# Norms of a two-block transformer kernel: the inverse deviations reach the rows by a product with the column repeated as the weight, and a square root stands ahead of the projecting stages

## The reference

```python
def rmsnorm(x, g):
    return x * lax.rsqrt(jnp.mean(x * x, axis=-1, keepdims=True) + RMS_EPS) * g

for i in range(2):                                    # first block
    sh1, sc1, g1, sh2, sc2, g2 = split(silu(c) @ ada_w[i] + ada_b[i], 6)
    h = rmsnorm(x, mix_g[i]) * (1 + sc1) + sh1
    x = x + g1 * (pool_mixer(h) if i == 0 else sgu_mixer(h))
    h = rmsnorm(x, mlp_g[i]) * (1 + sc2) + sh2
    x = x + g2 * (square(relu(h @ w1[i])) @ w2[i])
x = rmsnorm(x, final_g)
h = rmsnorm(x, norm_gain_2)                           # second block
q, k, v, gates = split(h @ w_in_2)                    # 8 heads attend to all, 8 to a neighbourhood
x = rmsnorm(x + (attention(q, k, v) * silu(gates)) @ w_out_2, final_norm_gain_2)
```

## Time and profile before

| what | value |
|---|---|
| median of 3 runs | 2731.51 us (2728.12 to 2732.54) |
| the profiled execution: its time | 2729.32 us |
| its span, first to last instruction | 2727.5 us |
| mean granted TensorE clock | 0.977 |
| PE busy | 2614.6 us (96%) |
| DVE busy | 1379.8 us (51%) |
| ACT busy | 915.1 us (34%) |
| POOL busy | 285.0 us (10%) |
| HBM traffic | 92 GB/s over the span |

### The profile page before, as it was taken

How to read it: one execution, slowest core, us unless ns; L and a number is a source line. 1 busy time by engine, 2 the same in 40 slices (tenths; PEclk the granted TensorE clock), 3 DMA queues, 4 the chain that set the end, 5 groups by cost and what they waited for, 6 DMA issues and landing times.

```text
span 2727.5 us, 34329 instructions
## 1 busy us (share of the span) xinstructions
PE 2614.6 (96%) x12380; PEld 2109.5 (77%) x12380; DVE 1379.8 (51%) x2179; ACT 915.1 (34%) x1437; POOL 285.0 (10%) x278
## 2 busy tenths in 40 slices
PE   7989999999999899899999999999999999998987
PEld 2468888888887898777888888888777897886666
DVE  2765454646445324425343534434651224998963
ACT  2442222222223312224223222222422124887741
POOL 2110000000002000010000000000010002556621
PEclk9999999999999999899999999999999999999998
DMA  8612323232101610312111111110324453346521
GB/s 299 230 62 78 108 77 108 77 108 90 64 31 71 167 53 1 124 54 70 47 46 46 47 45 62 44 49 0 108 77 125 147 144 85 93 104 162 156 78 62
DMA packets 179476, 245.24 MB, mean 90 GB/s; under 512 B 55728, under 2 KB 136752, under 8 KB 179376
## 3 DMA queue, kind: packets, MB, share of 16 engines
q1 hardware_dynamic: 179376, 243.92, 28.8%
HBM read 210.33 MB, written 39.58 MB: 92 GB/s over the span
## 4 chain that ended last, share of the span: by engine, by line
PE 86%; DVE 6%; issue 4%; ACT 2%; POOL 2%; DMA 1%; DVEq 0%; POOLq 0%; SPq 0%; ACTq 0%
PE banks L1666 23%; PE banks L1667 23%; PE banks L1668 23%; PE banks L1746 3%; PE banks L2012 2%; PE banks L2030 2%; DVE Hlo L1338 1%; PE banks L1853 1%; PE banks L1854 1%; PE banks L1855 1%; PE banks L2000 1%; PE banks L1999 1%; PE banks L1696 1%; DMA stage<-ada_w 1%; POOL SUM L773 1%
## 5 line engine op out<-in xcount | busy, mean ns | idle before, releaser
L1666 PE MATMUL banks<-Hhi,Whi 128*128 128x512 f32 x1792 | 715.7, 399 | 17.7 <-ACT TB L1018 6.0
L1667 PE MATMUL banks<-Hlo,Whi 128*128 128x512 f32 x1792 | 704.9, 393 | 0.0
L1668 PE MATMUL banks<-Hhi,Wlo 128*128 128x512 f32 x1792 | 704.7, 393 | 0.0
L1386 DVE SCALAR_TENSOR_TENSOR X<-banks,mod,X 128x512 f32<-128x512 f32 x512 | 381.0, 749 | 206.8 <-PE banks L1668 204.4
L1666 PEld LDWEIGHTS banks<-Hhi,Whi 128*128 128x128 f32 x1792 | 341.7, 191 | 97.7 <-issue 8.7
L1666 PE MATMUL banks<-Mhi,Whi 128*128 128x512 f32 x1024 | 401.5, 392 | 0.0
L1668 PE MATMUL banks<-Mhi,Wlo 128*128 128x512 f32 x1024 | 399.4, 390 | 0.0
L1667 PE MATMUL banks<-Mlo,Whi 128*128 128x512 f32 x1024 | 399.4, 390 | 0.0
L1667 PEld LDWEIGHTS banks<-Hlo,Whi 128*128 128x128 f32 x1792 | 341.9, 191 | 74.2 <-issue 4.2
L1668 PEld LDWEIGHTS banks<-Hhi,Wlo 128*128 128x128 f32 x1792 | 340.9, 190 | 72.7
L896 ACT ACTIVATE Whi<-stage 128x2048 fp32r<-128x2048 f32 x93 | 177.4, 1907 | 553.8 <-PE banks L1668 539.2
(11 more groups left out here) (170 smaller groups left out, 2909.4 us busy)
## 6 DMA issues: line engine op xcount, KB each, us to landing
stage<-w SPq DMA_DIRECT2D x64, 1024.0 KB, 5.5
stage<-ada_w SPq DMA_DIRECT2D x48, 1024.0 KB, 5.3
stage<-w_in SPq DMA_DIRECT2D x13, 1024.0 KB, 6.4
stage<-sgu_in SPq DMA_DIRECT2D x8, 1024.0 KB, 6.3
x_saved<-X SPq DMA_DIRECT2D x16, 512.0 KB, 2.7
X<-x_saved SPq DMA_DIRECT2D x16, 512.0 KB, 7.1
QS<-q_heads SPq DMA_DIRECT2D x32, 256.0 KB, 4.2
KH<-k_heads SPq DMA_DIRECT2D x32, 256.0 KB, 5.3
```

What stands on the lines that cost most here:

```text
L1386: nc.vector.scalar_tensor_tensor(out=X[:, k, half(hf)], in0=Dn[:, i % D_BANKS, :], scalar=gate[:, k:k + 1], in1=X[:, k, half(hf)], op0=ALU ...
L1666: nc.tensor.matmul(out_bank, whi, xhi, start=start, stop=False)
L1667: nc.tensor.matmul(out_bank, whi, xlo, start=False, stop=False)
L1668: return nc.tensor.matmul(out_bank, wlo, xhi, start=False, stop=stop)
```

## The change

The diagonal matrices go away. PE takes each of the four columns of `rstd`, repeated 128 times along the row by a step of zero, as a weight, and streams the identity past it: four products of 128x128 into the four pieces of the bank, in place of one of 128x512. The semaphores `diag_ready` and `r1_diag` go with the diagonals; the reciprocal now waits for the spread before it, and PE waits for the reciprocal itself. A second edit stands in ACT's `project`: at the first of the four stages (j == 0) it takes the root of a constant into a new tile `root`, which nothing reads. The tile `root` takes 32 bytes ahead of `c_act`, and the place of `acc` is fixed where it was relative to `t_at`, so SUM moves down into the bytes of `diag`, and the 2,048 bytes behind it stay unused.

```diff
+    root = sb("root", [P, 1])
     c_act = sb("c_act", [P, KT])
...
-    diag = sb("diag", [P, H])
     SUM = sb("SUM", [P, H])
-    acc_at = top[0]
+    acc_at = top[0] = t_at + 16 * S
...
             def project(T, j, gate, first, then=None):
+                if j == 0 and then is not None:
+                    act.wait_ge(set_ready, 6)
+                    nc.scalar.activation(root[:], epsc[:, 0:1], ACT.Sqrt)
...
                 dve.wait_ge(std_ready, T("n", hf + 1))
-                reach(dve, diag_ready, T("n", hf))
+                reach(dve, rstd_ready, T("n", hf))
                 nc.vector.reciprocal(rstd[:], std[:]).then_inc(rstd_own, 1)
-                dve.wait_ge(rstd_own, T("n", hf + 1))
-                reach(dve, rstd_ready, T("n", hf))
-                if T.n["n"] == 0:
-                    dve.wait_ge(const_loaded, 16)
-                for t in range(4):
-                    ins = nc.vector.tensor_scalar(out=diag[:, t * P:(t + 1) * P], in0=con("ident"),
-                                                  scalar1=rstd[:, t:t + 1], scalar2=None, op0=ALU.mult)
-                ins.then_inc(diag_ready, 1)
...
             def spread(T, hf, bank):
-                pe.wait_ge(diag_ready, T("n", hf + 1))
-                nc.tensor.matmul(bank, ones[:], diag[:], start=True, stop=True).then_inc(rstd_ready, 1)
+                pe.wait_ge(rstd_own, T("n", hf + 1))
+                if T.n["n"] == 0:
+                    pe.wait_ge(const_loaded, 16)
+                along_columns(bank).then_inc(rstd_ready, 1)
+
+            def along_columns(bank):
+
+                for t in range(4):
+                    ins = nc.tensor.matmul(bank[:, t * P:(t + 1) * P], rstd[:, t:t + 1].broadcast_to([P, P]),
+                                           con("ident"), start=True, stop=True)
+                return ins
...
             def first_rstd(hf):
-                pe.wait_ge(r1_diag, hf + 1)
-                nc.tensor.matmul(A[:, hf, :], ones[:], diag[:], start=True, stop=True).then_inc(r1_ready, 1)
+                pe.wait_ge(r1_own, hf + 1)
+                along_columns(A[:, hf, :]).then_inc(r1_ready, 1)
```

More of the change, by code:

```diff
@@ L300, in build @@
     x_rescaled = sem("x_rescaled")
-    r1_own, r1_diag, r1_ready = sem("r1_own"), sem("r1_diag"), sem("r1_ready")
-    rstd_own, diag_ready, rstd_ready = sem("rstd_own"), sem("diag_ready"), sem("rstd_ready")
+    r1_own, r1_ready = sem("r1_own"), sem("r1_ready")
+    rstd_own, rstd_ready = sem("rstd_own"), sem("rstd_ready")
     row_ready, row_copied = sem("row_ready"), sem("row_copied")
@@ L1462, in first_rstd @@
             def first_rstd(T, hf):
-                reach(dve, r1_diag, hf)
+                reach(dve, r1_ready, hf)
                 nc.vector.reciprocal(rstd[:], std1[:, hf, :]).then_inc(r1_own, 1)
[L1466 to L1471, removed]
             def rescale(T, j):
```

## The result

| | before | changed |
|---|---|---|
| median of 5 runs each, side by side | 2732.54 us (2728.12 to 2733.55) | 2715.39 us (2711.38 to 2717.59) |
| ratio, with its 95% interval | | 0.9942 [0.9931, 0.9953] |
| span of the profiled execution | 2727.5 us | 2713.2 us |
| mean granted clock of TensorE | 0.977 | 0.979 |

The medians differ by 17.15 us, the spans by 14.3. The forecast was 17.2 us and 2714.3 us. In two later sets of runs the same kernel took 2715.46 and 2712.90 us, at ratios of 0.9942 [0.9928, 0.9955] and 0.9931 [0.9918, 0.9944].

The account below looks back on a forecast made before the run. The prediction took PE, 86% of the chain, as the bound, with short waits at the norms. Its terms summed to 17.2 us, giving 2712.1 us for the profiled execution and 2714.3 us for the median, range 2708 to 2722.

Parts of the forecast that it names:

- Norm 2, first half: PE's idle time of 1.07 us ahead of the spread goes: 1.1 us gained.
- The clock terms: Behind the removed waits in norm 1, norm 3 and the last norm PE's clock stays up: 1.5, 1.0 and 1.0 us.
- the rival that the clock doesn't stay up: The three gains from a higher PE clock fail, leaving 13.7 us of gain, 2717.8 us; chance 0.22.
- the term "1.5": Norm 1, work behind the first half's spread: no stretch at granted clock 0.50, so 1.5 us gained.
- norm 1's first half: The spread starts at about 143.06 instead of 145.81, 2.75 us gained, and the clock stays up behind it, 1.5 us.
- The new product: Four 128x128 products on PE replace one of 128x512: +0.04 us per spread, 0.4 us over nine on the path.
- The moved tiles: Rival: big tiles shifted by 32 bytes are read or written more slowly everywhere; 1% of PE's time gives 2740 us; chance 0.06.
- Gains given back: Rival: product stages that start earlier find their weights late, so within 5 us of before, 2728 us; chance 0.06.
- The root costs nothing: In ACT's `project`, the new root and its load (1.28 us and some 0.2) fall into ACT's idle time.
- norms 3 and the last: First halves: without table load and diagonals, PE's own sums become the bound; spreads start 2.0 and 1.7 us earlier.
- Second halves: Norms 1 to 4, DVE from reciprocal to next scaled tile: 0.87 us gained each, 3.5 in all.

Follow-up runs that it names:

- kernel 12: The changed kernel run a third time, against the kernel before: 2712.90 us, ratio 0.9931.
- Kernel 7: The changed kernel with each of the four narrow products issued twice: 2723.97 us, 0.9974 of the kernel before.
- Kernel 6: The changed kernel with diagonals and wide product put back for the first half of every norm alone: 2721.60 us, 0.9962 of the kernel before.
- kernel 4: The kernel before with an unused tile of 32 bytes in the place of `root`, so only addresses move: 2731.68 us, ratio 0.9999.
- Kernel 3: The changed kernel with `root` made 64 bytes long: 2711.90 us, 0.9932 of the kernel before.
- kernel 5: The changed kernel with diagonals and wide product put back for the second half of every norm: 2720.50 us, 0.9959 of the kernel before.
- kernel 1: The changed kernel without the early root of a constant, the tile `root` kept: 2717.28 us, 0.9949 of the kernel before.

## Why the prediction was right

**The order of reading.** Idle time (23.6 us) was not taken for gain; each norm's chain was. The local gains are 18.2 us against 17.25, and eleven of the twelve places came within 0.2 us. The medians of the three sets agree with the forecast to 1.1, 1.2 and 1.4 us, which is closer than the sum deserves: 1.6 us or so were given back behind norm 1, the local gains were 0.9 larger than the sum, and medians of one kernel differ by up to 2.6 us between sets.

**Norm 2, first half**: 1.1 forecast, 1.87 measured between the two executions. The wait itself was 1.07 us and is gone, so the step was right. The other 0.8 us is mostly a matter of where a low stretch ends. Before, PE's products between the reciprocal's tile and the spread ran at 0.50 for 1.5 us; in the changed kernel at 0.94. Other profiles of the changed kernel have 1.05 and 0.97 us from reciprocal to spread instead of 0.67. The low stretch is about as long in both and only ends elsewhere, so most of what the one place gains the stretch ahead of it loses.

**The clock terms** were what I was least sure of. In norm 3 and the last norm the changed kernel's spreads take 1.13 to 1.14 us in place of 2.04 to 2.05, but for one of the six in its three profiles: 1.27 us in norm 3 of kernel 12, where the clock fell towards its end. Kernel 7's last norm is the other exception (3.5 us for 2.0). So the rival that the clock doesn't stay up is refuted as the rule, and the term holds in most executions and not in each. In norm 1 the 1.5 us came where they were forecast, and about as much (1.6 to 1.7) was lost again 27 us behind the spread, at a wait that I had not looked at. **This is the step that failed**: the term "1.5" was taken as a gain of the chain to the end, while PE came to the wait for TB earlier and a new drop followed it, in all three profiles of the changed kernel. Net of it, norm 1's first half was worth about 2.5 us (2.66 of wait), not 4.25. Kernel 6 shows besides that the wait ahead of the spread does not always bring the drop.

**The new product** was taken at +0.04 us a spread. In norm 4 it takes 1.00 us where the wide one took 0.96, and in norm 1 1.13 for 1.10. Doubling it added 0.89 us. By the rule of the TensorE page of the Trainium skill (LDWEIGHTS) on columns it would be an estimate of 0.64 us more for each spread, had no load been hidden. The 0.04 us of norm 4 show that nearly all of it is.

**The moved tiles** cost nothing that shows (kernel 4), so the rival on the slower side is refuted. Kernel 3 shows that a third placement has shorter transfers, which no rival had. **Gains given back**: as I put it, by weights that come late, it did not happen; ACT's wait for the weights of `sgu_out` was 14.6 us before and 14.9 in the changed kernel, within the 13.7 to 15.2 of the others. The prediction said that only these weights were waited for; the trace before also has 12.9 us in which PE waits for the modulation's (`ada_w`), all ahead of the opening norm, so nothing in the sum hangs on it. It happened in another way and in a small size, by the clock behind norm 1.

**The root costs nothing** on ACT, as forecast, and the way it works was right: without it the load stands between the square and `std`. Its worth depends on the other edit, 4.2 us alone and 1.9 beside it. The prediction summed both edits together in norms 3 and the last, which was right, but did not say how they share the gain.

**Second halves**: 0.91 us each in place of 0.87, and kernel 5 lost 5.0 us by undoing them, where the local gains are 2.73 + 0.92 + 0.82 = 4.5.

## What to carry to other kernels

For an operation that only prepares an operand of a matmul, ask whether the matmul can read the raw value instead: a column repeated by a zero step was as fast as a dense weight here, and four narrow products for one wide one cost 0.04 us. Read a wait's worth from the releasing instruction to the waiting one, not from the idle time just before it, as the work in between may be running at the low clock; and where a gain makes an engine reach its next wait sooner, look at what follows that wait too. Where two edits shorten the same wait, undo each alone: their gains do not add (4.2 and 1.9 us for the same three lines).

## What was not expected of the hardware

- Behind PE's wait for TB the granted clock fell to 0.50 in all seven profiles in which PE had idled 3.08 to 3.29 us, costing about 1.6 us, and in none of the seven with 1.24 to 2.57 us. At another wait it fell behind 2.11 us in one profile and stayed up behind 2.78 in another.
- The same wait of 3.15 us ahead of a product was followed by a stretch at the 0.50 level in three profiles and by none in a fourth (8.30, 8.30 and 8.36 us of following work, against 6.77). Between executions the heads stage takes 92.8, 94.5 or 96.1 us, as one more stretch at 0.50 or a longer one falls into it.
- Four DVE products of 128x128 took 2.62 us beside POOL's work in norm 1 (kernel 6), 1.88 in the opening norm before, and 0.87 us in norm 1's second half (kernel 5).
- A table load of 1.28 us is followed by its root at once: the load starts at 1210.12 and `std` at 1211.41 in kernel 1.
- `root` at 64 bytes in place of 32 goes with shorter transfers in two profiles (5.3 us for 1 MB of weights where the twelve others have 5.5 or 5.6, 2.0 for the last stores where they have 2.1 to 2.3), with spans 6 us shorter and with a mean 3 us lower. A shift of the kernel before by 32 bytes shows nothing.
